# Third kind of attention: the scores of two steps issued together at the head of every second step on TensorE

## The reference, cut to what matters

```python
s_c = jnp.einsum('bsgrd,bngd->bgrsn', qg, kc).astype(f32) * scale
p_c = jax.nn.softmax(jnp.where(valid_c, s_c, NEG), axis=-1) * valid_c
o_c = jnp.einsum('bgrsn,bngd->bsgrd', p_c.astype(vc.dtype), vc)
...
s = jnp.einsum('bqgrd,bgqnld->bgrqnl', qi, kg).astype(f32) * scale
s = jnp.where(mask[:, :, None], s, NEG)
p = jax.nn.softmax(s.reshape(sh[0], sh[1], sh[2], sh[3], -1), axis=-1).reshape(sh)
...
s_w = jnp.einsum('bcqgrd,bckgd->bcgrqk', qb, kb).astype(f32) * scale
p_w = jax.nn.softmax(s_w, axis=-1).astype(vb.dtype)
o_w = jnp.einsum('bcgrqk,bckgd->bcqgrd', p_w, vb).reshape(B, S, G, R, Dh)
...
o = g[..., 0, :] * o_c + g[..., 1, :] * o_s + g[..., 2, :] * o_w
```

## Time and profile before

| | before |
|---|---|
| median of 3 runs | 2524.25 us (2522.6 to 2525.85) |
| the profiled execution's own time | 2522.84 us |
| its span | 2521.0 us |
| TensorE busy | 2501.9 us, 99% |
| TensorE weight loads busy | 2023.9 us, 80% |
| VectorE busy | 1395.2 us, 55% |
| ScalarE busy | 943.7 us, 37% |
| granted TensorE clock, mean | 1.00 |

### The profile page before, as it was taken

One profiled execution on the slowest core, in us unless ns is written; L12 is line 12 of the kernel. 1 busy time (PEld: TensorE's weight loads), 2 busy tenths in 40 slices (PEclk: granted clock), 3 DMA queues, 4 the chain that ended last, 5 costly groups with the idle time before them and its releaser, 6 DMA issues.

```text
span 2521.0 us, 30069 instructions
## 1 busy us (share of the span) xinstructions
PE 2501.9 (99%) x11841; PEld 2023.9 (80%) x11841; DVE 1395.2 (55%) x1962; ACT 943.7 (37%) x1379; POOL 60.4 (2%) x77
## 2 busy tenths in 40 slices
PE   9999999999999999999999999999999999999999
PEld 7788888888888877888888888888777658888887
DVE  6556366645556655555663444566654676733433
ACT  5432334322334444223442232445544574422222
POOL 6000000000000000000001000000000001000000
PEclk9999999999999999999999999999999999999999
DMA  4222223444443311222343333222222111222222
GB/s 164 67 84 96 88 101 104 150 147 150 150 136 115 104 68 69 99 101 84 109 139 126 134 115 133 95 91 101 101 93 75 51 34 67 101 100 100 94 90 100
DMA packets 38629, 260.04 MB, mean 103 GB/s; under 512 B 4417, under 2 KB 4673, under 8 KB 8049
## 3 DMA queue, kind: packets, MB, share of 16 engines
q1 hardware_dynamic: 32976, 226.92, 26.2%
q10 hardware_dynamic: 5296, 30.20, 3.4%
q0 software_dynamic: 240, 1.28, 0.2%
HBM read 256.29 MB, written 2.10 MB: 102 GB/s over the span
## 4 chain that ended last, share of the span: by engine, by line
PE 94%; DVE 4%; ACT 1%; issue 1%; DMA 0%; SPq 0%; DVEq 0%; ACTq 0%
PE ps L2010 65%; PE ps L2037 9%; PE ps L2241 6%; PE ps L2063 5%; PE ps L2184 2%; PE ps L2225 2%; PE ps L2205 1%; PE ps L2467 1%; DVE w_lo L1139 1%; PE ps L2483 1%; PE ps L2163 0%; DVE a_lo L1263 0%; PE ps L2523 0%; PE ps L2329 0%; DVE T L1258 0%
## 5 line engine op out<-in xcount | busy, mean ns | idle before, releaser
L1139 DVE TENSOR_TENSOR w_lo<-raw,w_hi 128x2048 fp32r<-128x2048 f32 x208 | 477.5, 2295 | 325.1 <-ACT w_hi L570 275.3
L2010 PE MATMUL ps<-a_hi,w_hi 128*128 128x512 f32 x1408 | 550.4, 391 | 0.5 <-DVE w_lo L1139 0.3
L2010 PE MATMUL ps<-a_hi,w_lo 128*128 128x512 f32 x1408 | 547.9, 389 | 0.0
L2010 PE MATMUL ps<-a_lo,w_hi 128*128 128x512 f32 x1408 | 547.8, 389 | 0.0
L570 ACT ACTIVATE w_hi<-raw 128x2048 fp32r<-128x2048 f32 x198 | 376.4, 1901 | 404.0 <-PE ps L2010 338.2
L2010 PEld LDWEIGHTS ps<-a_hi,w_hi 128*128 128x128 f32 x1408 | 264.3, 188 | 57.2 <-issue 1.1
L2010 PEld LDWEIGHTS ps<-a_lo,w_hi 128*128 128x128 f32 x1408 | 264.4, 188 | 55.4 <-issue 1.0
L2010 PEld LDWEIGHTS ps<-a_hi,w_lo 128*128 128x128 f32 x1408 | 264.3, 188 | 54.8
L2010 PE MATMUL ps<-f_hi,w_hi 128*128 128x512 f32 x708 | 275.4, 389 | 0.0
L2010 PE MATMUL ps<-f_lo,w_hi 128*128 128x512 f32 x708 | 275.4, 389 | 0.0
L2010 PE MATMUL ps<-f_hi,w_lo 128*128 128x512 f32 x708 | 275.4, 389 | 0.0
(11 more groups left out here) (384 smaller groups left out, 3559.8 us busy)
## 6 DMA issues: line engine op xcount, KB each, us to landing
raw<-weights SPq DMA_DIRECT2D x209, 1024.0 KB, 4.9
ada_w<-ada ACTq DMA_DIRECT2D x24, 1024.0 KB, 4.9
merged<-cmp_w SPq DMA_DIRECT2D x2, 1024.0 KB, 5.8
out<-h SPq DMA_DIRECT2D x8, 256.0 KB, 2.0
h<-x_t SPq DMA_DIRECT2D x3, 512.0 KB, 7.1
raw<-weights SPq DMA_DIRECT2D x4, 256.0 KB, 5.1
kt<-c_row ACTq DMA_DIRECT2D x2, 512.0 KB, 3.6
pads<-p_t ACTq DMA_DIRECT2D x2, 512.0 KB, 4.0
```

The lines of the kernel that those rows point to most:

```text
L1139: dve.tensor_tensor(w_lo[n % 2][:, w], raw[n % 2][:, w], w_hi[n % 2][:, w].bitcast(F32), ALU.subtract)\
L2010: ins = pe.matmul(dst, a[i], b[j], start=done == 0, stop=done == total - 1)
```

## The change

The scores of steps s + 2 and s + 3 are both issued at the head of every even step s of the NSA attention, and none at the head of an odd one. Everything else, on every engine, stands where it stood. The other three attentions keep their order.

```diff
                 ahead = which > DEPTH
+                pairs = ahead
+
+                def next_scores(s):
+
+                    for i in ((s + 2, s + 3) if s % 2 == 0 else ()) if pairs else (s + 2,):
+                        if i < len(steps):
+                            scores(i)
                 for s in range(len(steps)):
-                    if ahead and s + 2 < len(steps):
-                        scores(s + 2)
+                    if ahead:
+                        next_scores(s)
                     for j in range(1 if diff else 2):
                         turn(s, j)
-                    if not ahead and s + 2 < len(steps):
-                        scores(s + 2)
+                    if not ahead:
+                        next_scores(s)
                     for at in plan[s]:
                         piece(*at)
```

## The result

The changed kernel takes 2529.76 us (median of 17 runs, 2527.97 to 2531.66) against 2524.41 us for the kernel before on the same chip (17 runs, 2522.6 to 2526.26). The ratio is 1.0022, 95% interval 1.0015 to 1.0028: slower, by 5.35 us, where the prediction had 3.1.

What follows compares the result with a forecast made beforehand. TensorE's own instructions and few waits were taken as the bound. Breaks -3.6, waits at heads +7.1, waits gone -1.3, new waits +0.9 gave +3.1 us on 2524.25, so 2527.3 us, range 2521.5 to 2531.5.

Steps and rivals of the forecast that it cites:

- within: Whole kernel: a time within about 0.2%, or 5 us, of the kernel before; chance 0.67.
- the second rival: At double blocks on TensorE: the break isn't saved and the waits are paid, +6.2 us, 2530.5 us; chance 0.18.
- The break, -3.6: Between joined score blocks on TensorE: each of seventeen double blocks saves 0.21 us of array emptying and refilling, -3.6 us.
- The waits at the heads, +7.1: At even steps' heads: TensorE waits for the exps of step s + 1 an iteration earlier than before, +7.1 us.
- I cost these at nothing: Heads 4 and 22: exps look late but should end ahead of the block, 0; 1.3 us for both otherwise.
- Waits that go and waits that are new, -1.3 and +0.9: Transposes of steps 15 and 34 wait less, -1.3 us; odd steps 1, 7 and 13 wait 0.3 each, +0.9 us.
- the third rival: At heads and wide steps: late copies delay the next exps in a chain, or the clock falls, +5 or more; chance 0.07.
- the first rival: At the heads: odd steps' exps come earlier, the waits don't come, only breaks count, -3.6 us, 2520.7 us; chance 0.17.

Runs made afterwards that it cites:

- e_fill: The changed kernel with four more matmuls of 384 columns, unread, at the head of step 26 ahead of the scores of step 28: 2528.52 us, ratio 1.0019.
- e_wait: The kernel before, single blocks, with a wait for the exps of step s + 1 behind the score block of every even step s: 2531.47 us, 1.0028.
- e_round: The changed kernel with ScalarE's three roundings of a weight unit one iteration later, VectorE's half left in place: 2537.21 us, ratio 1.0050.
- e_both_later: The changed kernel with ScalarE's rounding and VectorE's rest of the three weight units both one iteration later: 2527.59 us, ratio 1.0013.
- e_both_later0: The kernel before with ScalarE's rounding and VectorE's rest of the three weight units both one iteration later: 2527.70 us, ratio 1.0011.
- e_behind: The changed kernel with the double score block of every even step behind that step's transposes instead of ahead: 2532.51 us, ratio 1.0033.
- e_single_behind: The kernel before with the single score block of every step behind that step's transposes instead of ahead: 2552.82 us, ratio 1.0112.

## Why the prediction was right in kind and short in size

The direction, the mechanism and the place were right: the breaks are saved, the waits outweigh them, head 26 is the worst. The measured time lies inside the range; +5.35 us is just past the 5 us that the text drew as the border, where it had given 0.29, and "within" had 0.67. That the range reaches so far is owed to the second rival, a break that isn't saved anywhere, which is not what added the missing 2.3 us. TensorE's idle time in steps 1 to 34 rose from 4.7 to 115.40 - 105.92 = 9.5 us, between the bounds of 4.7 and 14 that the text had set, where its sum had 11.4:

```profile
1978.50:2093.90 115.40, 105.92 (x760) 68.43 (x759) 78.04 (x211) 80.84 (x238) 0.00 (x0) 0.99 0.11 38
```

By its own steps:

- **The break, -3.6.** Right per block: 1.06 and 1.49 us against 1.05 and 1.49. Wrong as a sum of 17, since eight of them lie under a wait; the next term pays for that. The rule of the Trainium skill ("TensorE: Matmul & The Clock Gate", section "Part 3: Packing small matmuls — row/col tiling"), by which the second block's loads would stand bare, isn't borne out between two blocks either: a bare load of 0.18 us would have made the 1.49 us a 1.67. (The paragraph above that rule in the same section also lets a load go ahead into a background weight buffer, which fits.)
- **The waits at the heads, +7.1.** Measured is each double block's length less what its columns need. That is 3.37 at head 26, 1.76 at 16, 1.58 at 8, 1.44 at 14, 0.65 at 4, 0.39 at 6, 0.38 at 24, 0.37 at 18, 0.28 at 2 and 0.11 at 12 and 20 together: 10.3, less the 1.3 that were there before, +9.0. The term was 1.9 us short. Two parts of it failed most. "I cost these at nothing" was wrong for head 4, 0.65 us (right for 22). And the waits were measured from the end of a single block, which for 128 columns comes 0.49 us after its start, while the columns take 0.21: the first term takes this break off, and the wait that covers it was counted here without it. That makes 0.23 to 0.32 us at each of the heads 8, 14, 16 and 26, 1.1 together. Heads 2, 6 and 24 took 0.75 more than their 0.3, and the predicted wait at head 32 (0.26 and the handover) didn't come.
- **Waits that go and waits that are new, -1.3 and +0.9.** Together -1.6, against -0.4 in the sum, is what the rest of the account leaves (5.36 + 3.6 - 9.0 - 1.55); it is a remainder and hides 1.2 us of what the waits and the clock add. Waits that are gone: 1.04 and 0.50 us at steps 15 and 34 (step 34 was costed at half), 0.23 each at 4 and 22, 0.14 at 7, and 0.17 and 0.14 ahead of values products, 2.45 in all. The new ones are at steps 1 (0.77 us, 0.17 before), 23 (0.46, 0.08 before) and 13 (0.34, 0.22 before), 1.1 more than before; at step 7, which the text had named, there is none. That is -1.35. TensorE after, at steps 1 and 23:

```profile
1979.85 0.33 PE L2205 MATMUL ps<-consts_sb,pads 128*128 128x128 f32 x1 [0.24 <-ACT T L676]
1980.71 0.30 PE L2205 MATMUL ps<-consts_sb,pads 128*128 128x128 f32 x1 [0.53 <-ACT pads L684]
...
2054.38 0.60 PE L2201 MATMUL ps<-consts_sb,pads 128*32 128x128 f32 x4 [0.46 <-DVE pads L1339]
```

- **The clock, 0 in the sum.** The step that failed in kind and not only in size: it stood only in the third rival (0.07 in all), as an addition of 3.1 us, although the same text expected a pause "of 3 us or more at head 26". `e_fill` puts it at 1.55 us. The Trainium skill ("TensorE: Matmul & The Clock Gate", section "Why this matters for your kernels") says that long idle gaps bring the clock back to half, and the trace agrees behind the pause of 3.09 us. Other runs here don't fit "long": the clock also fell behind pauses of 1.3 to 1.7 us (last section). The clock should have stood in the sum.
- **VectorE.** Its idle ahead of L1319 was to fall to about half of 21.6; it is 20.3 over the same 110 us of the attention. Instead ScalarE's wait for VectorE's factors fell, from 19.0 to 7.3 us. The same groups after, 1978.5 to 2088.5 us:

```profile
L1319 DVE TENSOR_TENSOR ps<-ps,consts_sb 128x256 f32<-128x256 f32 x37 | 15.9, 429 | 20.6 <-PE ps L2184 20.3
...
L684 ACT ACTIVATE pads<-pads,small 128x384 f32<-128x384 f32 (+3 forms) x29 | 15.7, 541 | 7.5 <-DVE small L1357 7.3
```

So the first rival's cause was there, 11.7 us less waiting on ScalarE, and yet the exps of odd steps came no earlier at heads 8, 14 and 16: those that head 8 waits for end 1.57 us after the head's start before, and 1.64 us after it with the change. What fits with it is that ScalarE starts each pair of steps later, since its copies wait for the transposes behind the double block; that was not tested by itself.

The account: breaks -3.6, waits +9.0, clock +1.55, the rest -1.6, sum +5.4. Its first two terms count from the columns alone, so the eight breaks under a wait stand in both, with opposite signs.

## What to carry to other kernels

Joining two blocks that run the array in the same form saves one break, but only where the second block's inputs are ready: lay the two engines' timelines side by side at every place, and join only at those (here five of 17, a small gain in place of a loss). A wait moved ahead of work that feeds the very engine it waits for is paid about in full, and it swallows the break that the joining was to save. And when a forecast contains new pauses of TensorE, put the clock into the sum: one fall cost 1.55 us here, and filling the pause of 3.09 us with work that nobody reads gave back half of what that head cost.

## What the hardware showed that was not expected

After pauses of 3.09 us (the change) and 3.03 us (`e_wait`) the clock went to its lower level for 3.4 and for 6.8 us; in the first case it fell only after TensorE had been back at work for a while, so the whole of it was paid. With the pause cut to 0.52 us by useless matmuls it did not fall.

The length of the pause alone doesn't decide it. Read in windows of 2 us over the attentions of the other runs, the clock also fell in or right behind pauses of 3.58 and 2.66 us (`e_round`), 2.79 (`e_both_later`), 1.70 and 0.46 close together (`e_both_later0`), 1.32 and 0.42 close together (`e_behind`) and 1.61, 1.47 and 1.47 (`e_single_behind`), each time for 3.4 or 6.8 us. It did not fall behind 2.58 us (`e_round`), nor behind 1.65, 1.65 and 1.66 (`e_single_behind`), nor behind the 1.04 us that is the longest pause of the kernel before in this stretch. TensorE in `e_round` at the transposes of step 15, and the 10 us from there on:

```profile
2034.64 0.63 PE L2209 MATMUL ps<-consts_sb,pads 128*128 128x128 f32 x4 [2.58 <-DVE pads L1367]
...
2034.00:2044.00 10.00, 7.87 (x63) 5.59 (x65) 6.67 (x18) 8.81 (x25) 0.00 (x0) 1.00 0.23 94
```

What decides besides the pause, no run here shows.
